# Two transformer blocks on one core: products with the identity and a gate row put into the waits of the norms, the token weights turned at an earlier norm, squares added on GpSimd, an operand swap in the S5 output, and another order of the first loads

## The reference

```python
h = layer_norm(concat([meta, x]), ln0_g, ln0_b)          # "ln0"
p = h @ w_in + b_in          # S5 input, q, k, v, gates
y_s5 = glu(gelu(s5_mixer(u)) @ s5_w_glu)   # diagonal state space model
hm   = head_norm(mlstm(silu(conv(qk)), v, i, f))
mix  = sigmoid(g_s5) * y_s5 + sigmoid(g_m) * ((sigmoid(o) * hm) @ m_w_out)
h = layer_norm(ALPHA*h + mix @ w_o, ...)                 # "n1"
h = layer_norm(ALPHA*h + relu(h @ w_up + b_up)**2 @ w_down, ...)   # "n2"
# second block
mod = silu(c) @ w_ada + b_ada        # shifts, scales, gates gt1, gt2
h = rmsnorm(x) * (1 + sc1) + sh1                         # "r1"
q, k, v, z = split(h @ w_in_2)
attn = attention(rope(rmsnorm(q)), rope(rmsnorm(k)), v)
u, v = split(gelu(z)); tok = u * (w_s @ rmsnorm(v) + b_s)    # w_s: 8 x 128 x 128
x = x + gt1 * (concat([rmsnorm(attn), rmsnorm(tok)]) @ w_out_2)
h = rmsnorm(x) * (1 + sc2) + sh2                         # "r2"
x = x + gt2 * conv_glu_ffn(h);  out = rmsnorm(x, g_final)
```

## Time and profile before

| | |
|---|---|
| three runs | 776.25 us median, 775.84 to 779.43 |
| profiled execution | 780.67 us, its span 778.9 us |
| busy, share of the span | TensorE 96%, DVE 74%, ACT 60%, GpSimd 17% |
| mean granted TensorE clock | 0.988 of full |
| DMA | 148.54 MB, 191 GB/s |

### The profile page before, as it was taken

How to read it: one execution, slowest core, us unless ns; L and a number is a source line. 1 busy time by engine, 2 the same in 40 slices (tenths; PEclk the granted TensorE clock), 3 DMA queues, 4 the chain that set the end, 5 groups by cost and what they waited for, 6 DMA issues and landing times.

```text
span 778.9 us, 14473 instructions
## 1 busy us (share of the span) xinstructions
PE 749.8 (96%) x5361; PEld 685.1 (88%) x5361; DVE 575.6 (74%) x853; ACT 464.5 (60%) x776; POOL 134.5 (17%) x139
## 2 busy tenths in 40 slices
PE   5989999999999989999999998999999999999996
PEld 4989999888999878998988987998878999999994
DVE  6897888754777468787575667887788899866675
ACT  4867775557775455555455545667776555555554
POOL 5000000000124113233232220000002222243321
PEclk9999999999999999999999999999999999999998
DMA  8364333245355688788787881763236765556541
GB/s 291 119 182 163 131 115 109 82 111 188 111 187 164 207 296 284 243 316 300 261 267 282 273 312 36 255 259 108 66 105 209 235 232 184 192 187 195 182 136 54
DMA packets 46151, 148.54 MB, mean 191 GB/s; under 512 B 9340, under 2 KB 10108, under 8 KB 46096
## 3 DMA queue, kind: packets, MB, share of 16 engines
q1 hardware_dynamic: 44544, 144.88, 54.9%
q10 hardware_dynamic: 1552, 2.91, 1.1%
HBM read 145.64 MB, written 1.05 MB: 188 GB/s over the span
## 4 chain that ended last, share of the span: by engine, by line
PE 87%; DVE 7%; ACT 4%; issue 1%; DMA 1%; DVEq 0%; POOL 0%; SPq 0%; ACTq 0%
PE ps L763 31%; PE ps L713 21%; PE ps L488 18%; PE ps L504 3%; PE ps L1007 1%; DVE wl L1627 1%; PE ps L727 1%; PE ps L580 1%; ACT wh L1084 1%; PE ps L949 1%; PE ps L595 1%; DMA vtk<-in_x 1%; PE ps L917 1%; PE ps L931 1%; PE ps L647 0%
## 5 line engine op out<-in xcount | busy, mean ns | idle before, releaser
L1627 DVE TENSOR_TENSOR wl<-raw,wh 128x1024 fp32r<-128x1024 f32 x220 | 282.7, 1289 | 106.7 <-ACT wh L1084 105.8
L1084 ACT ACTIVATE wh<-raw 128x1024 fp32r<-128x1024 f32 x220 | 231.6, 1054 | 63.3 <-PE ps L713 49.8
L763 PE MATMUL ps<-xh,wh 128*128 128x256 f32 x672 | 190.4, 283 | 1.7 <-DVE taps L2288 1.3
L763 PE MATMUL ps<-xl,wh 128*128 128x256 f32 x672 | 188.6, 281 | 0.0
L763 PE MATMUL ps<-xh,wl 128*128 128x256 f32 x672 | 188.6, 281 | 0.0
L763 PEld LDWEIGHTS ps<-xh,wh 128*128 128x128 f32 x672 | 127.0, 189 | 6.8 <-issue 2.5
L763 PEld LDWEIGHTS ps<-xl,wh 128*128 128x128 f32 x672 | 127.0, 189 | 1.9
L763 PEld LDWEIGHTS ps<-xh,wl 128*128 128x128 f32 x672 | 127.1, 189 | 0.0
L488 PE MATMUL ps<-xh,wh 128*128 128x256 f32 (+1 forms) x400 | 116.9, 292 | 1.9 <-POOL xl L2353 1.1
L488 PE MATMUL ps<-xh,wl 128*128 128x256 f32 (+1 forms) x400 | 113.4, 284 | 0.0
L488 PE MATMUL ps<-xl,wh 128*128 128x256 f32 (+1 forms) x400 | 113.2, 283 | 0.0
(11 more groups left out here) (400 smaller groups left out, 1250.4 us busy)
## 6 DMA issues: line engine op xcount, KB each, us to landing
raw<-in_w_stream SPq DMA_DIRECT2D x220, 512.0 KB, 3.7
ada_w<-in_w_ada SPq DMA_DIRECT2D x48, 512.0 KB, 6.0
vtk<-in_x SPq DMA_DIRECT2D x2, 512.0 KB, 4.7
out<-ob SPq DMA_DIRECT2D x4, 256.0 KB, 2.0
u<-uT SPq DMA_DIRECT2D x16, 34.0 KB, 2.2
eepp<-in_s_mats SPq DMA_DIRECT2D x1, 512.0 KB
bti<-btr SPq DMA_DIRECT2D x16, 32.0 KB, 2.6
zv<-in_ln_rows ACTq DMA_DIRECT2D x1, 512.0 KB, 6.0
```

Of the source, the lines that this page charges most:

```text
L763: mm = nc.tensor.matmul(ps[:, bank, 0:SEQ], w, x, start=(k == 0), stop=(k == 3 * KD - 1))
L1084: nc.scalar.activation(wh[:, b % RING], raw[:, b % RING], ACT.Identity).then_inc(hi_done, 1)
L1627: V.tensor_tensor(wl[:, b % RING], raw[:, b % RING], wh[:, b % RING].bitcast(F32), ALU.subtract).then_inc(lo_done, 1)
```

## The change

- The start: the learned tokens are loaded and measured first, the identity is loaded by itself and the rest of the constants after the second block. 9 identity products in place of 10. All eight `turn_x` stand ahead of `first_blocks`. ACT normalises the tile `xt[2]`, DVE the other two and two small columns for ACT.
- S5 output: data and matrix swap roles, so each of the 12 products loads 64 columns of weights and moves 128 columns, two of them on the two halves of the array's columns. The result lies the other way round: ACT copies it to `std` (`s5_rows`), TensorE turns it with two turns one block later (`turn_s5`), and ACT copies it to `y4` another block later.
- n1: six identity products between the turns of the two row tiles; `ws` is loaded earlier and turned right after them; ACT's two copies stand after its split.
- r1: `gate_row` stands behind `last_rows`, in banks 2 and 3, with 17 identity products ahead of it; six products between the turns. The copies of the row stand where those of `ws` stood. The turns of `ws` and the 19 identity products around them are gone.
- Token branch: GpSimd adds the four squared tiles (three additions of 128 x 256), `tok_ms` takes 2 products.
- End: ACT runs a square root on one spare column ahead of the gate's copies.

The lines below are in this order: SP, TensorE, ACT, GpSimd.

```diff
+            sp.dma_start(xt[0][0:META, :], A["meta_tokens"]).then_inc(S["meta_landed"], 16)
             sp.dma_start(xt[1], A["x"][0, 0:P, :]).then_inc(S["x_landed"], 16)
             sp.dma_start(xt[2], A["x"][0, P:2 * P, :]).then_inc(S["x2_landed"], 16)
-            sp.dma_start(xt[0][0:META, :], A["meta_tokens"]).then_inc(S["meta_landed"], 16)
-            sp.dma_start(cst[:, :], A["consts"]).then_inc(S["consts_landed"], 16)
+            sp.dma_start(ident, A["consts"][:, C_ID:C_ID + P]).then_inc(S["ident_landed"], 16)
             for b in range(RING):
                 sp.dma_start(raw[:, b], A["w_stream"][b]).then_inc(landed[b], 16)
+                if b == 1:
+                    sp.dma_start(cst[:, C_ONE:NCONST], A["consts"][:, C_ONE:NCONST]).then_inc(S["consts_landed"], 16)
...
-            for k in range(4):
+            for k in range(KD):
                 turn_x(k)
-            first_blocks(B_U, (0, 1), lambda k: (LN["lo"], k + 1), 0, lambda k: turn_x(k + 4) if k < 4 else None)
+            first_blocks(B_U, (0, 1), lambda k: (LN["lo"], k + 1), 0)
...
-                n = SEQ // STEP
-                for q in range(4):
-                    o, s = ps[:, 4, q * n:(q + 1) * n], 4 * c + q
-                    for part, cp in enumerate((cpr, cpi)):
-                        nc.tensor.matmul(o, cp[:, s, 1:STEP + 1, :].rearrange("p b h -> p (b h)"), xst[:, part, q, :],
-                                         start=(part == 0), stop=False)
-                    mm = nc.tensor.matmul(o, toep[:, s, :], u4[:, s, MCK:NCK], start=False, stop=True)
+                for pair in range(2):
+                    for k in range(3):
+                        for g in range(2):
+                            q = 2 * pair + g
+                            if k < 2:
+                                x, w = xst[:, k, q, :], (cpr, cpi)[k][:, 4 * c + q, 1:STEP + 1, :].rearrange("p b h -> p (b h)")
+                            else:
+                                x, w = u4[:, 4 * c + q, MCK:NCK], toep[:, 4 * c + q, :]
+                            mm = nc.tensor.matmul(ps[64 * g:64 * g + 64, 4, pair * P:(pair + 1) * P], x, w,
+                                                  start=(k == 0), stop=(k == 2), skip_group_check=True)
                 mm.then_inc(S["s5_y"], 1)
+
+            def turn_s5(c):
+
+                pe.wait_ge(S["s5_rows"], c + 1)
+                if c == CH - 1:
+                    pe.wait_ge(S["s5_free"], CH)
+                for pair in range(2):
+                    mm = nc.tensor.transpose(ps[:, S5_BANK[c], SEQ + pair * P:SEQ + (pair + 1) * P], std[:, pair * P:(pair + 1) * P], ident)
+                mm.then_inc(S["s5_turned"], 1)
...
                 if (h, t) == (1, 0):
-                    pe.wait_ge(S["y4_ev"], CH)
+                    pe.wait_ge(S["s5_rows"], CH)
+                    pe.wait_ge(S["y4_ev"], CH - 1)
...
-            turn_normed("n1", (ln("n1", "norm_act"), ln("n1", "norm_act", 2), ln("n1", "norm"), ln("n1", "norm_act", 3)))
+            turn_normed("n1", (ln("n1", "norm_act"), ln("n1", "norm_act", 2), ln("n1", "norm"), ln("n1", "norm_act", 3)), (6, 7))
+            pe.wait_ge(S["ws_landed"], 16)
+            for n in range(2):
+                for q in range(4):
+                    mm = nc.tensor.transpose(ps[:, 2 + n, q * P:(q + 1) * P], ws[:, 4 * n + q, :], ident)
+                mm.then_inc(S["ws_turned"], 1)
...
+            last_rows(B_IN2 - 2, [(gh[:, j % 4, :], gl[:, j % 4, :]) for j in (KF - 2, KF - 1)], F1_BANKS, lambda k: (S["f_lo"], KF - 1 + k))
+
+            pe.wait_ge(S["centred"], 2)
+            keep_running(17, 0)
             pe.wait_ge(S["mod_done"], ADA_LOOP)
-            gate_row(1, KD)
-            last_rows(B_IN2 - 2, [(gh[:, j % 4, :], gl[:, j % 4, :]) for j in (KF - 2, KF - 1)], F1_BANKS, lambda k: (S["f_lo"], KF - 1 + k))
-
-            pe.wait_ge(S["row_ev"], 2)
-            keep_running(8, 4)
             pe.wait_ge(S["centred"], 4)
-            pe.wait_ge(S["mixing_landed"], 64)
-            for n in range(2):
-                for q in range(4):
-                    mm = nc.tensor.transpose(ps[:, 2 + n, q * P:(q + 1) * P], ws[:, 4 * n + q, :], ident)
-                mm.then_inc(S["ws_turned"], 1)
-            keep_running(4, 4)
-            pe.wait_ge(S["y_second"], 2)
-            keep_running(7, 4)
-            turn_normed("r1", (ln("r1", "norm_act"), ln("r1", "norm_act", 2), ln("r1", "norm"), ln("r1", "norm_act", 3)))
-            keep_running(3, 1)
+            gate_row(1, KD, 2)
+            turn_normed("r1", (ln("r1", "norm_act"), ln("r1", "norm_act", 2), ln("r1", "norm"), ln("r1", "norm_act", 3)), (6, 0))
+            keep_running(3, 0)
...
+            act.wait_ge(S["x2_scale"], 1)
+            nc.scalar.activation(xt[2], xt[2], ACT.Identity, bias=lnr[:, 2, 1:2], scale=lnr[:, 2, 0:1]).then_inc(LN["norm"], 1)
...
+                if b - 1 in S5_OUT_AT:
+                    s5_rows(S5_OUT_AT.index(b - 1))
+                if b - 2 in S5_OUT_AT:
+                    y4_copy(S5_OUT_AT.index(b - 2))
                 evac(b)
...
+            nc.scalar.activation(std[:, 0:1], eps[:, 0:1], ACT.Sqrt)
...
+            for k in range(2):
+                pool.wait_ge(S["tok_sq"], 2 * k + 2)
+                G.tensor_tensor(sq[:, QT + 1 + k, :], sq[:, 2 * k, :], sq[:, 2 * k + 1, :], ALU.add).then_inc(S["tok_pairs"], 1)
+            pool.wait_ge(S["tok_pairs"], 2)
+            G.tensor_tensor(sq[:, QT, :], sq[:, QT + 1, :], sq[:, QT + 2, :], ALU.add).then_inc(S["tok_sum"], 1)
```

More of the change, by code:

```diff
@@ L732, in last_rows, with turn_normed @@
                             mm.then_inc(S["quarter_summed"], 1)
[L734 removed]
+            def turn_normed(tag, ready, between=None):
                 for t in range(NT):
+                    if t and between:
+                        keep_running(*between)
                     for half in range(2):
@@ L1372, in _ @@
             hi(B_IN2 - 2 + AHEAD)
-            for half in range(2):
-                act.wait_ge(S["row_mm"], half + 1)
-                nc.scalar.activation(gate1[:, half * 512:(half + 1) * 512], ps[:, 6 + half, :], ACT.Identity, scale=float(D))\
-                    .then_inc(S["row_ev"], 1)
             def square_sum(src, to):
```

71 lines of the change are left out of this document (41 added, 30 removed).

## The result

| | median, us | runs |
|---|---|---|
| before | 777.79 (775.84 to 779.43) | 9 |
| after | 771.92 (769.48 to 774.47) | 9 |

The ratio is 0.9927, with a 95% interval of 0.9907 to 0.9947. The gain is 5.9 us. The forecast was 11.0 us, and its range ended at 770.5, 1.4 us short of the measured median.

What follows compares the result with a forecast made beforehand. TensorE was taken to hold 87% of the chain. Terms 1.7 + 2.7 + 3.6 + 1.3 + 0.2 = 9.5 us without the clock, plus 1.5 of clock, 11.0 us off, gave 765.2 us from the median 776.25; range 760.5 to 770.5.

Steps and rivals of the forecast that it cites:

- the median of the runs is 776.25, 4.4 us lower; against it the same sum: Last step: the 11.0 us taken off the profiled 780.67 was also taken off the median, giving 765.2 us.
- Start, 1.7: Kernel's start: tokens measured first and turns ahead of the first product, which ends at 23.5 us; 1.7 us saved (0.5 to 2.7).
- the first product after 17 us: Sign at the kernel's start: the prediction is wrong if the first product starts after 17 us; it was placed near 16.0.
- S5, 2.7: S5 outputs: TensorE gets 2.7 of its 4.7 us (0.6 to 4.7); 2 us go into a wait ahead of head 2's numerators.
- n1, 1.2 where the clock holds: Norm after the output projection: identity products and `ws` turns fill TensorE's wait; 1.2 us saved, nothing if the clock falls.
- r1, 3.6: Token mixing's norm: gate row behind the sum (1.72 us) and new order; product 3.6 us sooner, 1.7 if identity products hold up turns.
- Token branch, 1.3: Token branch: two products in place of eight save 1.3 us on TensorE, with GpSimd's sum hidden.
- The clock at the scores: Scores after the token branch: the clock fall at 531.35 cost 1.9 us and may not recur, since the small work shrinks.
- End, 0.2: Kernel's end: the 1.28 us table leaves the chain, but DVE's scalings then stand there; 0.2 us saved (0 to 0.6).
- The clock, of which I took 1.5: Clock term at n1 and the scores: 1.2 + 1.9 = 3.1 us, of which half, 1.5, was counted.
- the clock is lost on turns: Rival, chance 0.14: turns don't count as busy; n1 gives 0, start 0.5, token branch's clock nothing; 8.3 us, 768.

Runs made afterwards that it cites:

- r1_old_look: The changed kernel with the whole order of before at r1, the same kernel as r1_old; a single execution for another trace, 773.51 us.
- r1_old_again: The changed kernel with the whole order of before at r1, the same kernel as r1_old, run again; median 773.69 us, ratio to before 0.9948.
- turns_between: The changed kernel with the turns of x's blocks 4 to 7 put back between the first gate's u groups; median 773.49 us, ratio to before 0.9947.
- no_ident: The changed kernel without the identity products at n1 and r1; median 772.78 us, ratio to before 0.9932.
- r1_old: The changed kernel with the whole order of before at r1, turns of `ws` included; median 775.12 us, ratio to before 0.9957.

## Why the prediction was wrong

**The step that failed** is the last of the sum: "the median of the runs is 776.25, 4.4 us lower; against it the same sum". The sum fitted the profiled pair (11.0 forecast, 10.5 measured), with misses among its terms that cancelled. That pair was one of the slowest executions of before, with four falls of the clock, and one of the fastest after, with one fall and a clock that rose in time at the start. Compare executions without a fall: 774.9 us before, 769.0 to 769.5 after (the changed kernel's lowest). That is 5.4 to 5.9 us. It is the gain of the work itself, to be held against my 9.5 "without the clock".

By its terms, with falls priced apart:

- *Start, 1.7.* 1.5 where the clock holds. The condition that I wrote down, the first product after 17 us, came true in five of the eleven traces with nine products and turns in a row, where 24 turns took 6.74 us. My worst case for it, "0.5 if the clock falls in the turns", was too mild: the v turn is then at 39.65 to 41.11 us, from level with before's 39.75 to 1.4 us later. Over all executions the start gives nothing (0.9996, 0.9975 to 1.0018).
- *S5, 2.7.* 3.3. Both waits are where they were placed, but TensorE's is 0.66 us long and not 2; y4's late copy was its cause.
- *n1, 1.2 where the clock holds.* 1.3. The rival in which turns give the clock nothing didn't come true here.
- *r1, 3.6.* 3.5 in the profiled pair, the product at 473.52 and 10.2 us behind the sum. But I counted it as free of the clock. 1.5 of it is the gate row (forecast 1.72). Of the rest, 2.0, the fall has 1.6 to 2.0 by the estimates above, and the fastest executions of before didn't have it. Free of the clock the term is 1.5 to 1.9, and it is the one that was mis-sized most, by about 2 us.
- *Token branch, 1.3.* Wrong sign: 0.5 lost. I asked whether GpSimd's sum would be in time and it was, by 2.5 us. I didn't ask who works beside GpSimd, and I took TensorE to be the bound where DVE, with the sums still on TensorE, had 0.05 us of slack. The clock at the scores, where I hoped for 1.9, fell in ten of the fifteen traces of the changed kernel and its variants, and a fall there is worth 1.0 us in the old code (38.3 against 37.3), not 1.9.
- *End, 0.2.* 0.25.

Without the clock these are 1.5 + 3.3 + 1.5 - 0.5 + 0.25 = 6.05 us, or up to 0.4 more with the order at r1; between executions without falls 5.4 to 5.9 were measured, and the difference isn't placed. From 9.5 to 6.05 it is 2.1 at r1, 1.8 at the token branch, 0.2 at the start, less 0.6 at S5. The clock, of which I took 1.5, then gives back little. The median lies 2.9 us above the executions without a fall before (777.79 against 774.9), and 2.4 to 2.9 us above them after: falls are fewer, but in many executions the start costs up to 4.5 us more than in the best ones.

Of my rivals, "the clock is lost on turns" (768) had the right place for the start, though not the right cause. The Trainium skill, "TensorE: Matmul & The Clock Gate", Part 4, PE-mode transpose, would have the eight turns in a row at the lower clock each time. In r1_old_look and r1_old_again the kernel, the place and the load's arrival (7.12 and 7.16 us) are the same, and the turns take 4.31 us in one and 6.74 in the other. So the trace of r1_old_look doesn't agree with the rule as it is worded: all 24 turns ran at the upper level. And in turns_between, with turns between the products, which are full matmuls, the clock was low as well. Whether turns count less than matmuls isn't shown by that; something that differs from one execution to the next decides too.

What stays open: why the clock rises or falls in one execution and not in the next; how 14 products bring an early rise, if they do; and the old order at r1 without a fall.

## What to carry to other kernels

A sum made against one profiled execution holds for that execution. Before it is carried over to a median, look at where the profiled time stands among the times, count the falls of the clock in the trace, and take the falls' price out of every term, also out of stretches where idle or filler work ran at the lower clock and looks like an order's cost. When work moves to GpSimd, look at what DVE does in that moment, and whether TensorE is really the bound there; a row of the old trace where the two overlap has the price. And at a kernel's start look up when the clock first rose, before reading a mean clock near 1.00 as full speed.

## What the hardware showed that was not expected

- A fall of the clock lasted 3.4 or 6.8 us. One of 3.4 us cost 1.0 us at the scores before and 1.3 after (39.2 against 37.9), 1.3 at n1 and 1.5 at the start; the one of 6.8 at no_ident's scores cost 2.6 (40.5 against 37.9). Two executions of the kernel before, with four falls and with none, lie 5.8 us apart.
- The record of the granted clock starts with the first rise, at 9.9 to 22.95 us. Until then the windows read 1.00 also where 24 turns took 6.74 us instead of 4.3. The times of the changed kernel so don't follow its mean recorded clock (774.47 us at 0.996, 772.65 at 0.992), while those of before do. At the start the durations tell, and the time of the first entry.
- GpSimd's addition of 128x256 held a two-input DVE operation back by 0.54 us, and the old trace has 48 low parts that ended 1.08 to 1.15 us behind a GpSimd operation that was running when they began.
- Two executions, one each of r1_old and no_ident, ran at a granted clock of 0.75 from end to end and took 912 and 911 us.
